# Sums of squares by accumulating transfers: GpSimd's adds of three norms become DMAs from SBUF to SBUF

## The reference

```
rms_norm(x, g) = x * rsqrt(mean(x*x, -1) + 1e-6) * g
```

## Time and profile before

| | |
|---|---|
| Time, median of 3 runs (lowest, highest) | 2315.44 us (2314.51, 2316.42) |
| Span of the profiled execution, first to last instruction | 2314.4 us, 38060 instructions |
| TensorE busy, and its weight loads | 2286.0 us (99%), 1990.8 us (86%) |
| VectorE busy | 1486.3 us (64%) |
| ScalarE busy | 1281.1 us (55%) |
| GpSimd busy | 108.4 us (5%) |
| Granted TensorE clock, mean | 0.999 of full speed |
| Moved by DMA | 419.21 MB, mean 181 GB/s |

### The profile page before, as it was taken

How to read it: one execution, slowest core, us unless ns; L and a number is a source line. 1 busy time by engine, 2 the same in 40 slices (tenths; PEclk the granted TensorE clock), 3 DMA queues, 4 the chain that set the end, 5 groups by cost and what they waited for, 6 DMA issues and landing times.

```text
span 2314.4 us, 38060 instructions
## 1 busy us (share of the span) xinstructions
PE 2286.0 (99%) x13068; PEld 1990.8 (86%) x13068; DVE 1486.3 (64%) x1762; ACT 1281.1 (55%) x1590; POOL 108.4 (5%) x89
## 2 busy tenths in 40 slices
PE   7999999999999999999999999999999999999998
PEld 5888888888888888888888888888888888888887
DVE  6577666666666655556666666686666666654443
ACT  5555466666666644445554555556666666654443
POOL 4122100000000000000000000010000000000000
PEclk9999999999999999999999999999999999999999
DMA  6554555555555555555555555555555555555554
GB/s 237 185 164 157 189 187 185 181 188 185 189 183 188 183 189 183 190 183 196 167 172 171 163 163 172 165 168 187 189 183 189 182 188 183 182 189 187 186 186 132
DMA packets 115477, 419.21 MB, mean 181 GB/s; under 512 B 12832, under 2 KB 12960, under 8 KB 115168
## 3 DMA queue, kind: packets, MB, share of 16 engines
q1 hardware_dynamic: 114192, 413.43, 54.8%
q0 software_dynamic: 512, 2.95, 0.3%
q10 hardware_dynamic: 720, 2.10, 0.2%
HBM read 416.33 MB, written 2.10 MB: 181 GB/s over the span
## 4 chain that ended last, share of the span: by engine, by line
PE 96%; DVE 2%; POOL 1%; issue 1%; ACT 1%; DMA 0%; DVEq 0%; ACTq 0%; POOLq 0%
PE acc L1008 58%; PE acc L1009 29%; PE acc L1012 3%; PE acc L1011 2%; DVE X L736 1%; POOL vsum L402 1%; PE sc_ps L1146 0%; PE sc_ps L1126 0%; PE sc_ps L1133 0%; DVE w_lo L720 0%; DMA h<-x_t 0%; PE sc_ps L1141 0%; PE sc_ps L1125 0%; PE misc L1117 0%; PE acc L1190 0%
## 5 line engine op out<-in xcount | busy, mean ns | idle before, releaser
L1008 PE MATMUL acc<-X,w_hi 128*128 128x512 f32 x4200 | 1505.1, 401 | 18.2 <-DVE X L736 13.3
L720 DVE TENSOR_TENSOR w_lo<-raw,w_hi 128x1024 fp32r<-128x1024 f32 x784 | 965.1, 1237 | 546.3 <-ACT w_hi L439 545.7
L1009 PE MATMUL acc<-X,w_lo 128*128 128x256 f32 x4200 | 1182.8, 282 | 0.0
L439 ACT ACTIVATE w_hi<-raw 128x1024 fp32r<-128x1024 f32 x784 | 825.1, 1058 | 477.1 <-PE acc L1009 371.2
L1008 PEld LDWEIGHTS acc<-X,w_hi 128*128 128x128 f32 x4200 | 791.8, 189 | 199.5 <-issue 10.9
L1009 PEld LDWEIGHTS acc<-X,w_lo 128*128 128x128 f32 x4200 | 796.9, 190 | 12.1
L1008 PE MATMUL acc<-hid,w_hi 128*128 128x512 f32 x1376 | 487.5, 397 | 0.0
L1009 PE MATMUL acc<-hid,w_lo 128*128 128x256 f32 x1376 | 387.4, 282 | 0.0
L1008 PEld LDWEIGHTS acc<-hid,w_hi 128*128 128x128 f32 x1376 | 258.9, 188 | 62.2
L1009 PEld LDWEIGHTS acc<-hid,w_lo 128*128 128x128 f32 x1376 | 258.5, 188 | 1.4
L449 ACT ACTIVATE hc<-acc 128x512 f32<-128x512 f32 x104 | 62.1, 597 | 164.5 <-PE acc L1012 164.4
(11 more groups left out here) (157 smaller groups left out, 1329.0 us busy)
## 6 DMA issues: line engine op xcount, KB each, us to landing
raw<-w_stream SPq DMA_DIRECT2D x784, 512.0 KB, 3.4
out<-out_sb SPq DMA_DIRECT2D x8, 256.0 KB, 2.9
h<-x_t ACTq DMA_DIRECT2D x3, 512.0 KB, 7.2
WS<-ws_t POOLq DMA_DIRECT2D x1, 1024.0 KB, 5.3
BS<-bs_row POOLq DMA_DIRECT2D x1, 1024.0 KB, 8.2
mask<-mask_d POOLq DMA_DIRECT2D x1, 576.0 KB, 4.4
h<-x_t ACTq DMA_DIRECT2D x2, 256.0 KB, 4.7
rope<-rope_d POOLq DMA_DIRECT2D x1, 256.0 KB, 3.2
```

The source lines that it names most:

```text
L439: nc.scalar.activation(w_hi[slot][:, :], raw[slot][:, :], ACT.Copy).then_inc(hi_ready, 1)
L720: nc.vector.tensor_tensor(w_lo[slot][:, :], raw[slot][:, :], w_hi[slot][:, :], ALU.subtract)\
L1008: nc.tensor.matmul(bank, hi, moving[:, kt, :], start=first, stop=False)
L1009: op = nc.tensor.matmul(bank[:, S:2 * S], lo, moving[:, kt, 0:S], start=False, stop=False)
```

## The change

In norms 1, 2 and 3 each addition of `sq` to `ssum` is issued as a DMA that reads `sq`, adds it to `ssum` and writes `ssum`, all in SBUF. It is issued by GpSimd's queue and raises a new semaphore, `ss_moved`, by 16. All who waited for the addition wait for this semaphore: GpSimd before the next transfer, ScalarE before the next pair, TensorE before the mean. Norms 0 and 4 keep their instructions and count in `ss_added` alone, from lower values. The loop over pairs on GpSimd and the loop over a_w_out on ScalarE are written out.

```diff
@@ norm_sums on GpSimd
                 nc.gpsimd.memset(ssum[:, :], 0.0).then_inc(ss_clear, 1)
                 pool.wait_ge(ss_clear, n + 1)
-                with pool.Fori(0, pairs) as i:
+                for i in range(pairs):
                     pool.wait_ge(squared, pairs * (n - 1) + POOL_PAIRS + 1 + i)
-                    pool.wait_ge(ss_added, pairs * n + i)
-                    nc.gpsimd.tensor_tensor(ssum[:, :], ssum[:, :], sq[:, :, :].rearrange("p a b -> p (a b)"),
-                                            ALU.add).then_inc(ss_added, 1)
+                    wait_pos(pool, ss_moved, 16 * (pairs * (n - 1) + i))
+                    pool.dma_start(ssum[:, :], sq[:, :, :].rearrange("p a b -> p (a b)"), accum_op=ALU.add)\
+                        .then_inc(ss_moved, 16)
@@ norm 4 on GpSimd (and likewise in residual, last_block and the end of TensorE's work)
-                pool.wait_ge(ss_added, NORM_PAIRS * 4 + i)
+                pool.wait_ge(ss_added, NORM_PAIRS + i)
@@ norm_pair on ScalarE
-                wait_pos(act, ss_added, NORM_PAIRS * n + pr)
+                wait_pos(act, ss_moved, 16 * NORM_PAIRS * (n - 1) + 16 * pr)
@@ ScalarE's loop over a_w_out
-            with act.Fori(0, KT // 4) as i:
+            for i in range(KT // 4):
                 for s in range(4, 12):
@@ mean_square on TensorE
-                pe.wait_ge(ss_added, NORM_PAIRS * (n + 1))
+                if n == 0:
+                    pe.wait_ge(ss_added, NORM_PAIRS)
+                else:
+                    pe.wait_ge(ss_moved, 16 * NORM_PAIRS * n)
```

More of the change, by code:

```diff
@@ L251, in trunk @@
         ss_added = sem("ss_added")
+        ss_moved = sem("ss_moved")
         ms_ready = sem("ms_ready")
@@ L483, in residual @@
                 else:
-                    act.wait_ge(ss_added, NORM_PAIRS * n + pr)
+                    act.wait_ge(ss_added, NORM_PAIRS + pr)
                     for b in range(2):
@@ L493, in last_block @@
                 if b == 0:
-                    act.wait_ge(ss_added, NORM_PAIRS * 5 - 1)
+                    act.wait_ge(ss_added, NORM_PAIRS * 2 - 1)
                 kt = KT - 2 + b
@@ L1230, in _ @@
             turn_four(1)
-            pe.wait_ge(ss_added, NORM_PAIRS * 5)
+            pe.wait_ge(ss_added, NORM_PAIRS * 2)
             pe.wait_ge(squared, NORM_PAIRS * 4 + POOL_PAIRS + 1)
```

## The result

The changed kernel takes 2321.86 us (2320.88 to 2322.62) where the one before takes 2315.04 (2314.09 to 2316.42): ratio 1.0029, with a 95% interval from 1.0019 to 1.0039, or 6.8 us more. The forecast was 2322. The profiled execution has a span of 2320.9 us and took 2322.62.

The account below looks back on a forecast made before the run. TensorE, busy 99% of the span, was taken as the bound, with the stage after w_o deciding. 7 x (5.25 - 4.10) - 1.4 = +6.65 us on 2315.44 gave 2322.1 us, range 2313.8 to 2338.

Parts of the forecast that it names:

- (a): ScalarE waits for the previous pair's transfer before making the next X; cover 9.9 us after a_w_out, 4.0 after w_o.
- The gain of 1.4 us: After w_o: without GpSimd's additions VectorE's round falls below TensorE's and TensorE's 1.38 us wait goes, -1.4 us.
- R: Transfer's round trip, from the end of sq on ScalarE to the semaphore read there; 5.25 us expected, 3.35 to 8.4 bounds.
- The point of 4.10 us: After w_o: the longest round trip without a stall of TensorE; above it every pair adds the excess.
- The base from rope: Round-trip term from the nearest row, rope's 256 KB on the same queue: 3.2 us from issue to landing.
- The adding's reading and writing: Round-trip terms for reading the destination, 0.7 us, and writing it only after that, 0.7 us again.
- The hand-overs between engines: Round-trip term from the end of sq on ScalarE to GpSimd's start: 0.15 us.
- Sharing with the weights: Round-trip term for sharing engines with weight loads, which land in 3.9 us in this stage against 3.4 overall: 0.5 us.
- rival 1: The transfer is hidden, its round trip under 4.3 us: not slower, 2314.0 to 2315.4 us, chance 0.25.
- The formula: After w_o, over the 7 intervals between 8 pairs: change = 7 x (R - 4.10) - 1.4 us.
- TensorE's wait of 8 us at the hand-over: Sign to be seen: TensorE waiting for x_low about 8 us after 1550 instead of 1.4.
- rival 2: GpSimd can't make transfers while VectorE is busy, or adding is itself slow: 2330 to 2347.8 us, chance 0.22.

Follow-up runs that it names:

- 1: Changed kernel with only norm 3, after w_o, summed by transfers; norms 1 and 2 keep GpSimd's additions: 2321.31 us, ratio 1.0028 to the kernel before.
- 2: Changed kernel with norms 1 and 2 by transfers and norm 3 by GpSimd's additions: 2315.09 us, ratio 1.0001 to the kernel before.
- 8: Changed kernel, but in norms 1 and 3 ScalarE waits for the last transfer before sq, not before X: 2313.70 us, ratio 0.9996 to the kernel before.
- 3: Kernel before, with norm 3's eight GpSimd additions covering 8 of 512 columns, the rest left out: 2313.05 us, ratio 0.9992.
- 6: Changed kernel with weight loads after the first four units cut to 128 of 1024 columns: 2315.21 us; the kernel before with such loads took 2316.86.
- 9: Kernel before, with norm 3's eight additions moved from GpSimd to VectorE, behind x_low: 2313.04 us, ratio 0.9991.
- 7: Changed kernel with plain copies of sq over ssum instead of adding transfers: 2318.54 us, ratio 1.0014 to the kernel before.
- 11: Changed kernel run once more, unaltered, for a second profile: 2321.08 us.
- 12: Kernel before run once more, unaltered, for a second profile: 2315.24 us.
- experiment 4: Changed kernel with a second buffer for norm 3's squares, ScalarE waiting for the transfer of two pairs back: 2320.19 us, ratio 1.0023 to the kernel before.

## Why the prediction was right, point by point

- **The place and the mechanism: right.** Only (a) after w_o binds (1, 2), and X stands behind the wait (8). The later means and the other norms cost nothing.
- **The gain of 1.4 us: right.** Where R is short or the adds are gone the stage falls from 51.1 to 49.5 us: 3, 6, 8 and 9 give 1.5 to 1.7.
- **The point of 4.10 us: right to 0.1.** R of 3.85 costs nothing (6). In 7, R is 4.52 and the stage grows by 3.2 us, 1.1 of them clock: 7 x (4.52 - 4.10) - 1.4 = +1.5, against 2.1. Both 7 and the changed kernel would fit 4.0 us.
- **R = 5.25 us: close, measured 4.98, and that by luck,** for the terms erred both ways: 1.3 us too much in two of them, 1.0 too little in the other two. The base from rope, 3.2, should have been 2.3 (a copy within SBUF, 7). The adding's reading and writing, 1.4, is 1.0. The hand-overs between engines, 0.15, are 0.55: 0.30 from sq's end to GpSimd's issue, and 0.25 from the landing to X, which rope's row does not hold. Sharing with the weights, 0.5 and constant, is a mean of 1.1: nothing for three transfers, 1.4 to 1.6 for three, 3.5 for the first. The three other terms as measured make 3.85 us, under the point of 4.10: without the sharing the change would be rival 1, a gain. In the forecast's own sum this term didn't decide (4.75 us without it gives +3.2); the adding and the base, both too large, stood in for what the weight loads really cost. The weights' own lateness, 3.9 against 3.4 us, said what the traffic does to a load, not to a transfer that meets three of them.
- **The formula: right to 0.4 us.** 7 x (4.98 - 4.10) - 1.4 = +4.8; the stage grew by 5.2.
- **TensorE's wait of 8 us at the hand-over: mis-sized.** 5.7 us in all; 3.5 at the hand-over and 1.8 before it, for w_lo. The late rounds also reached the weights through w_hi and w_lo, queued behind X, which I had named but not priced.
- **Two x_low at 0.98 us: right. X 6.7 us apart: 6.43. Landing 5.1 us: a mean of 4.4** over the seven that X waits for.
- **Not predicted: the clock.** 6.8 us less 5.2 leaves 1.6. The three profiles with the wait of 3.5 us at the hand-over (after, 1, 11) lost 1.65, 2.2 and 1.1 us to half clock, a mean of 1.65, and the three comparable ones without it (before, 12, 2) nothing. The sizes agree, but the mean is over three single profiles, and the part in the changed kernel's first profile arose at 148 us, ahead of any change in the work. (So there the forecast's sign "the stages before 1100 us as long as now to 0.3 us" missed; in 11 it held.) That runs with the long wait have the lower clock is shown by the clocks of all runs above; where in an unprofiled run it fell is not on record, so the size of this share stays an estimate. The forecast's nearness owes something to it: the stage alone would have made 2315.0 + 5.2 = 2320.2.
- **Rival 1 fell** to the weights' traffic, **rival 2** to experiment 6: the adding alone is 1.0 us, VectorE no hindrance.

## What to carry to other kernels

Before an addition becomes a transfer, compare its round trip with the slack at the place with the least of it, and take the landing that it has beside the other traffic there, not the quiet one: the long ones (up to 6.8 us here) make the mean of 4.4 that decides, while the median over the kernel is 3.3. Put a wait in front of the instruction that needs it; eight us hung on X standing behind a wait that only sq needed (experiment 8). A second buffer did not help where the transfers themselves followed one another (experiment 4); an engine that gets slack back from the change itself may be the better place for the work (experiment 9).

## What the runs showed of the hardware

- 256 KB from SBUF to SBUF on GpSimd's queue: 2.3 us copied, 3.3 accumulated, alone; up to 5.3 and 7.4 beside 512 KB weight loads.
- A GpSimd addition of 128x512 lengthens two of VectorE's x_low from 0.87 to 1.92 us, with a start inside it; accumulating transfers leave them at 0.98.
- The granted clock fell to 0.50 behind TensorE's wait of 1.76 us at 148 us in 3 of 14 profiles, and behind waits of 3.0 to 3.5 us at the hand-over in 3 of 4, for 1.1 to 2.2 us of loss each; behind waits of 1.4 us or less there it fell in none of ten.
